# Second mixer's scores as two 64-row products in two accumulator banks, with the values' product first in each slot

## Chip, cores and metric

The kernel runs on one core of a Trainium2 chip. The metric is the device time of one execution in microseconds, taken as the median of several runs. A profiled execution of the same program gives the span and all rows shown here.

## What is computed

A trunk of two layers on a sequence of 256 tokens with 2048 channels, in fp32. Layer 0 has two parallel mixers in one projection (a gated linear recurrence, and 16 heads of windowed attention of 64 channels each), layer 1 has differential attention; after each comes a gated feed-forward part. The layer that the change is about, cut from the reference:

```python
q = z[..., :qk_w].reshape(bsz, seq, C_HEADS, 2, C_QK)        # 16 heads, 2 maps, 64 channels
k = z[..., qk_w:2 * qk_w].reshape(bsz, seq, C_HEADS, 2, C_QK)
v = z[..., 2 * qk_w:].reshape(bsz, seq, C_HEADS, C_V)        # C_V = 128
s = jnp.einsum('bqhje,bkhje->bhjqk', qblk, k)                # one score matrix per map j
p = jax.nn.softmax(s, axis=-1)
att = p[:, :, 0] - lam * p[:, :, 1]
return jnp.einsum('bhqk,bkhe->bqhe', att, v)
```

## The kernel before

**Large products.** Every weight block of 512 x 512 passes through two forms: ScalarE writes its high part (`hi`, line 1051), VectorE the rest (`lo`, line 1791). TensorE then forms three products (high by high, low by high, high by low). A *slot* is one such block: two halves (one per tile of 128 tokens) of 12 products of 512 columns, 24 in all (`product`, line 1461, matmul on line 1477). The two banks of each of two accumulator pairs `acc` take turns.

**Order of the work.** `make_plan` writes one list of tasks, and each engine's program walks through that list and picks out what is its own, so the list is the order on TensorE, VectorE, ScalarE, GpSimd and the load queue alike. `run` (line 332) makes for each slot: the first half, `early` tasks, `hi` and `lo` of blocks to come, in the output projection an `add_output` per half (VectorE adds the product to the sum in SBUF, lines 1909 and 1911), the second half, and then the `post` tasks.

**Attention within the slots.** `mixer_slots` (line 204) spreads the heads over slots. A group has 8 of them, i = 0 to 7. In layer 0 there are 2 groups (16 heads); in layer 1 there are 4 groups, and one i is one head for one tile of 128 queries, so 32. For each i, three slots one after the other hold its steps on TensorE: the score (`s0`) in slot start + i, the transposes of the softmax weights (`pt`) one slot later, the values' product (`pv`) two slots later. The groups start at slots that lie 10 apart in layer 0 and 10 or 12 apart in layer 1; the last group of either layer lies in the slots of the output projection. Lines 260 to 265 give the order within a slot:

```python
for s in range(len(slots)):
    for kind, lag in (("s0", 0), ("pt", 1), ("pv", 2), ("s", 0)):
```

**The steps of layer 1.** The score is one product (line 1590): the stationary operand is 128 rows of queries (64 channels of map 0, 64 of map 1), and the moving one is 128 rows by 512 columns of keys, where map 0's keys stand in the upper 64 rows of the first 256 columns and map 1's in the lower 64 rows of the last 256, with zeros in the other two quarters (`keys`, zeroed by GpSimd, line 2312). It fills the bank `sc`. VectorE takes the maximum of both maps in one reduce (line 1927) and scales it (line 1929); ScalarE forms the two exponentials from `sc` into `prob` (line 1152) and counts `exp_done`; VectorE divides and subtracts the maps (`difference`, early in the next slot, lines 1937 to 1942). `pt` transposes `prob`, ScalarE copies that to `probT` (line 1164), `pv` multiplies it with the values into 128 columns of the bank `pv` (line 1619), and VectorE copies these out (line 1961, counts `o_done`). ScalarE squares them for the norm of the head (line 1174).

**The steps of layer 0.** The score is two products of 256 columns, one per tile of queries, both in `sc` (line 1586). VectorE adds the log counts and takes the maximum (line 1922, counts `s_free`). The values' product is 4 small products (line 1614); VectorE takes a reciprocal (line 1953) and scales twice into `tok` (line 1956, the second counts `o_done`).

**What a score waits for.** On TensorE a score waits for `exp_done` (layer 1) or `s_free` (layer 0) of the head before, so that `sc` has been read. A values' product waits for the copy to `probT` and for `o_done` of the head before. An fp32 product appears in the trace as two weight loads and two matmul records; a transpose as one.

**Other users of the two banks.** `sc` and `pv` are also used by the recurrence's gates, by the transposes at the boundaries between parts and by the feed-forward blocks (`corner`, `upper`, line 807); for these nothing changes.

Of the kernel before, what the change touches and what calls it, by code (L numbers as in the profile page):

```python
# [183 lines left out]
class Plan:  # L184
# [3 lines left out]
    def __init__(self):  # L188
        self.u = self.n = self.e = self.m = self.heads = self.ropes = 0
        self.stats = self.squares = self.updates = self.xm = 0  # L190
        self.y_gains, self.y_counts = {"pool": 0, "dve": 0}, {}
        self.source = {}
        self.ready, self.read, self.pt, self.parts = {}, {}, {}, []
        self.stat, self.update, self.squared, self.y_gained = {}, {}, {}, {}
        self.bodies = 0
        self.place, self.after, self.heads_of, self.head_units, self.x_read, self.wholes, self.last_body = {}, {}, [], [], [], {}, []
        self.last_ups = []

# [5 lines left out]
def mixer_slots(plan, layer):  # L204
# [53 lines left out]
    if layer == 1:  # L258
        starts[0] = evacs["k", 0].s + 3
    for s in range(len(slots)):  # L260
        for kind, lag in (("s0", 0), ("pt", 1), ("pv", 2), ("s", 0)):
            for g, start in enumerate(starts):
                i = s - start - lag
                if 0 <= i < HEADS_OF_GROUP:
                    task = put(s, kind=kind, g=g, i=i, n=plan.heads + HEADS_OF_GROUP * g + i, v_group=evacs["v", g].n)
                    if kind == "pt" and layer == 1:
                        slots[s].early.append(Task("difference", n=task.n))
# [184 lines left out]
def number(plan, tasks):  # L452

    for task in tasks:
        if task.kind == "T":
            task.e = plan.e
            plan.e += 1
            if task.src != "x":
                plan.read["tok" if task.src == "tok" else "stage", task.t] = task.e
            key = {"x": ("x", task.b), "tok": ("y", task.layer)}.get(task.src, (task.src, task.layer))  # L460
            plan.ready[(*key, task.g, task.t)] = task.e
            plan.source[(*key, task.g, task.t)] = task
            if task.src == "tok":
                task.m = plan.m
                plan.m += 1
            if task.src == "x":
                task.m = plan.xm
                task.update = plan.update.get((task.b, task.g, task.t))
                plan.xm += KT
        elif task.kind == "pt":  # L470
            task.e = plan.e
            plan.e += 1
            plan.pt[task.n] = task.e
        elif task.kind in ("rms_x", "rms_y"):
            task.stat, task.sq = plan.stats, plan.squares
            plan.stat[task.kind, task.b, task.t] = plan.stats
            plan.stats += 1
        elif task.kind in ("square", "y_square"):
            task.sq, task.update = plan.squares, plan.update.get((task.b, task.c, task.t))
            task.stat = plan.stat.get(("rms_x", task.b - 1, 0))  # L480
            plan.squares += 1
            if task.kind == "y_square":
                plan.squared[task.b, task.slot.cb, task.t] = plan.squares
        elif task.kind == "y_gain":
            task.sq, task.gained = plan.squared[task.b, task.c, task.t], plan.y_gains[task.what]
            plan.y_gained[task.b, task.c, task.t] = task.what, plan.y_gains[task.what]
            plan.y_gains[task.what] += 1
            plan.y_counts[task.b] = dict(plan.y_gains)
        if task.kind in ("evac", "silu"):
            task.stat = plan.stat["rms_x", task.b, 0]  # L490
        if task.kind == "update":
            if task.b:
                task.stat, task.update = plan.stat["rms_y", task.b, task.t], plan.updates
                task.m = plan.y_gained[task.b, task.c, task.t]
                plan.update[task.b, task.c, task.t] = plan.updates
                plan.updates += 1
        if task.kind in ("evac", "update", "pv", "s", "silu", "gate_up"):
            task.tok_free = [plan.read.get(("tok", t)) for t in range(NT)]
            task.stage_free = [plan.read.get(("stage", t)) for t in range(NT)]
        if task.kind == "s":  # L500
            task.prev_pt = plan.pt.get(task.n - 1)
        if task.kind == "half" and not task.slot.recurrent:
            region, kg = task.slot.lhs
            key = ("x", task.slot.b) if region == "h" else ("y", task.slot.layer)
            if region == "h" and task.slot.b == 0:
                task.m, task.hi = KT * (kg + 1), "xT"
            elif task.slot.w == "down":
                task.e, task.m = task.slot.block_e + task.t, task.slot.block_m + task.t
            else:
                turn = plan.source[(*key, kg, task.t)]  # L510
                task.e, task.m, task.hi = turn.e, turn.m, turn.src
# [118 lines left out]
def trunk(nc, x, norm_mix_pre, norm_mix_post, norm_ffn_pre, norm_ffn_post,  # L630
# [9 lines left out]
    with ExitStack() as ctx:  # L640
# [78 lines left out]

        acc = [[ctx.enter_context(nc.psum_tensor(f"acc{i}{t}", [P, KC], F32)) for t in range(NT)] for i in range(2)]  # L720
        tp = [ctx.enter_context(nc.psum_tensor(f"tp{i}", [P, KT, P], F32)) for i in range(2)]
        sc = ctx.enter_context(nc.psum_tensor("sc", [P, 2, T], F32))
        pv = ctx.enter_context(nc.psum_tensor("pv", [P, 2, T], F32))


        landed = [sem(f"landed{i}") for i in range(BLOCK_RAW)]
# [292 lines left out]
        def _(act):  # L1019
# [119 lines left out]
            def softmax(task):  # L1139
                n = task.n  # L1140
                act.wait_ge(nmx_done, n + 1)
                if n >= 2:
                    act.wait_ge(o_done, n - 1)
                if task.layer == 0:
                    for t in range(NT):
                        ins = act.activation(prob[:, t, :], prob[:, t, :], ACT.Exp, scale=SCALE, bias=nmx[:, t:t + 1],
                                             accum_out=den[n % 2][:, t:t + 1])
                    ins.then_inc(exp_done, 1)
                else:
                    act.wait_ge(tp_done, task.prev_pt + 1)  # L1150
                    for m in range(2):
                        ins = act.activation(prob[:, m, :], sc[:, m, :], ACT.Exp, scale=SCALE, bias=nmx[:, m:m + 1],
                                             accum_out=den[n % 2][:, m:m + 1])
                    ins.then_inc(exp_done, 1)

# [278 lines left out]
        def _(pe):  # L1434
# [75 lines left out]
            def task_of(task):  # L1510
# [60 lines left out]
                elif task.kind == "s0":  # L1571
                    n = task.n
                    if n > 16:
                        pe.wait_ge(exp_done, n)
                    elif n:
                        pe.wait_ge(s_free, n)
                    else:
                        pe.wait_ge(rg_act, RG_ACT * (AT - 1) + 4)
                    if task.i == 0:
                        for src in "qk":  # L1580
                            for t in range(NT):
                                wait_event(pe, plan.ready[src, task.layer, task.g, t])
                    q, k, kt = qT[task.g % 2], keys[task.g % 2], task.i // 2
                    if task.layer == 0:
                        for t in range(NT):
                            mm = pe.matmul(sc[:, t, :], q[:, kt, t * P:(t + 1) * P], k[:, kt, task.i % 2, :],  # L1586
                                           start=True, stop=True)
                    else:
                        t = task.i % 2
                        mm = pe.matmul(sc[:, :, :].rearrange("p m t -> p (m t)"), q[:, kt, t * P:(t + 1) * P],  # L1590
                                       k[:, kt, :, :].rearrange("p m t -> p (m t)"), start=True, stop=True)
                    mm.then_inc(s_done, 1)
                elif task.kind == "pt":
                    if task.layer == 0:
# [7 lines left out]
                elif task.kind == "pv":  # L1602
                    n = task.n
                    wait_event(pe, plan.pt[n])
                    if n:
                        pe.wait_ge(o_done, n)
                    if task.i == 0:
                        for t in range(NT):
                            wait_acc(pe, task.v_group, t)
# [152 lines left out]
        def _(dve):  # L1762
# [150 lines left out]
            def softmax(task):  # L1913
# [4 lines left out]
                if task.layer == 0:  # L1918
                    if n:
                        dve.wait_ge(tp_done, task.prev_pt + 1)  # L1920
                    for t in range(NT):
                        ins = dve.tensor_tensor_reduce(prob[:, t, :], sc[:, t, :], logc[:, t, :], 1.0, 3.0 * NEG,
                                                       ALU.add, ALU.max, mx[:, t:t + 1])
                    ins.then_inc(s_free, 1)
                    dve.wait_ge(s_free, n + 1)
                else:
                    dve.tensor_reduce(mx, sc[:, :, :], AX.X, ALU.max).then_inc(max_part, 1)
                    dve.wait_ge(max_part, n - 16 + 1)
                dve.tensor_scalar(nmx, mx, -SCALE, None, ALU.mult).then_inc(nmx_done, 1)

# [467 lines left out]
```

## Time and profile before

| | |
|---|---|
| Median of 3 runs | 2159.02 us (2158.26 to 2159.08) |
| The profiled execution's own time | 2158.62 us |
| Its span in the trace | 2156.8 us, so 1.8 us lie around it |
| TensorE busy | 2141.2 us (99%), 9771 matmuls |
| VectorE busy | 1698.2 us (79%) |
| ScalarE busy | 1489.6 us (69%) |
| GpSimd busy | 230.7 us (11%) |
| Read from memory | 416.92 MB, 196 GB/s over the span |

Layer 0's heads run from about 199 to 341 us, layer 1's from 1141 to 1435 us. Busy time of TensorE is the sum of its matmul records; these overlap (a record lasts from the entry of its first column to the exit of its last), so a duration there is longer than the step from one matmul to the next. The chain of waits, in which each piece ends where the next begins, shows the steps.

### The profile page before, as it was taken

How to read it: one execution, taken by the hardware profiler on the slowest of the kernel's cores; microseconds unless marked ns; L12 is line 12 of the kernel's file. 1: busy time of each engine (PE TensorE's matmuls, PEld its weight loads, DVE VectorE, ACT ScalarE, POOL GpSimd, SP SyncE). 2: the span in 40 equal slices, each digit the busy share in tenths (PEclk: the TensorE clock that was granted, in tenths of full speed). 3: DMA queues.
4: the chain of work that ended last, by engine and by line, in shares of the span. 5: the costliest groups of instructions: out<-in, count | busy, mean ns of one | idle time of the engine just before them, and what ended most of it. 6: DMA issues, size and time to landing. Idle time of an engine off the chain costs nothing.

```text
span 2156.8 us, 26554 instructions
## 1 busy us (share of the span) xinstructions
PE 2141.2 (99%) x9771; PEld 1765.4 (82%) x9771; DVE 1698.2 (79%) x1538; ACT 1489.6 (69%) x1774; POOL 230.7 (11%) x274
## 2 busy tenths in 40 slices
PE   9999999999999999999999999999999999999998
PEld 7888888888888888888887787788888888888886
DVE  5577466898898888888755656678998888888886
ACT  6677544787777777777655555447777777777774
POOL 0851000000000000000021001001000000000001
PEclk9999999999999999999999999999999999999999
DMA  9545445799989999997564454557999999998993
GB/s 315 189 154 194 145 148 198 255 290 298 266 256 263 282 296 276 285 289 230 183 215 146 149 169 143 177 175 239 278 299 273 275 292 279 281 292 266 263 263 149
DMA packets 226559, 508.82 MB, mean 236 GB/s; under 512 B 13736, under 2 KB 16384, under 8 KB 214656
## 3 DMA queue, kind: packets, MB, share of 16 engines
q1 hardware_dynamic: 214192, 422.68, 55.6%
q0 software_dynamic: 11520, 83.89, 19.7%
q8 instruction: 79, 1.29, 0.2%
q10 hardware_dynamic: 720, 0.56, 0.1%
q14 instruction: 48, 0.39, 0.0%
HBM read 416.92 MB, written 6.29 MB: 196 GB/s over the span
## 4 chain that ended last, share of the span: by engine, by line
PE 95%; DVE 2%; issue 1%; ACT 1%; DMA 1%; SPq 0%; ACTq 0%; POOLq 0%; POOL 0%; DVEq 0%
PE acc L1477 34%; PE acc L1696 20%; PE sc L1490 20%; PE pv L1490 10%; PE acc L1490 5%; PE tp L1504 3%; PE sc L1590 1%; DVE w_lo L1791 1%; PE pv L1619 1%; PE sc L1586 1%; PE pv L1614 1%; DMA raw<-in_ev_w_in 0%; PE sc L1569 0%; PE pv L1569 0%; ACT h_hi L1097 0%
## 5 line engine op out<-in xcount | busy, mean ns | idle before, releaser
L1791 DVE TENSOR_TENSOR w_lo<-raw,w_hi 128x2048 fp32r<-128x2048 f32 x263 | 601.6, 2293 | 100.2 <-PE acc L1477 41.5
L1051 ACT ACTIVATE w_hi<-raw 128x2048 fp32r<-128x2048 f32 x263 | 503.7, 1916 | 120.4 <-PE acc L1477 45.6
L1477 PE MATMUL acc<-w_hi,h_hi 128*128 128x512 f32 x936 | 261.4, 401 | 2.6 <-ACT h_hi L1021 2.6
L1477 PE MATMUL acc<-w_lo,h_hi 128*128 128x512 f32 x936 | 252.2, 391 | 0.2
L1477 PE MATMUL acc<-w_hi,h_lo 128*128 128x512 f32 x936 | 251.1, 390 | 0.0
L1791 DVE TENSOR_TENSOR w_lo<-xs,w_hi 128x2048 fp32r<-128x2048 f32 x88 | 201.2, 2288 | 31.3 <-PE acc L1696 20.4
L1477 PEld LDWEIGHTS acc<-w_lo,h_hi 128*128 128x128 f32 x936 | 175.6, 188 | 38.9 <-DVE w_lo L1791 1.4
L1477 PEld LDWEIGHTS acc<-w_hi,h_lo 128*128 128x128 f32 x936 | 175.5, 188 | 37.0
L1477 PEld LDWEIGHTS acc<-w_hi,h_hi 128*128 128x128 f32 x936 | 171.1, 189 | 37.0 <-issue 5.5
L1051 ACT ACTIVATE w_hi<-xs 128x2048 fp32r<-128x2048 f32 x88 | 168.5, 1915 | 23.9 <-PE acc L1490 8.1
L1317 ACT ACTIVATE yacc<-acc 128x512 f32<-128x512 f32 x160 | 95.0, 595 | 113.3 <-PE acc L1696 113.3
L1696 PE MATMUL acc<-w_hi,y_lo 128*128 128x512 f32 x640 | 171.0, 389 | 0.0
L1696 PE MATMUL acc<-w_hi,y_hi 128*128 128x512 f32 x640 | 171.0, 389 | 0.0
L1696 PE MATMUL acc<-w_lo,y_hi 128*128 128x512 f32 x640 | 171.0, 389 | 0.0
L1791 DVE TENSOR_TENSOR w_lo<-gq,w_hi 128x2048 fp32r<-128x2048 f32 x54 | 123.5, 2288 | 24.4 <-PE acc L1696 19.6
L1696 PEld LDWEIGHTS acc<-w_hi,y_hi 128*128 128x128 f32 x640 | 120.1, 188 | 24.9
L1696 PEld LDWEIGHTS acc<-w_lo,y_hi 128*128 128x128 f32 x640 | 120.1, 188 | 24.9
L1696 PEld LDWEIGHTS acc<-w_hi,y_lo 128*128 128x128 f32 x640 | 120.1, 188 | 24.9
L1791 DVE TENSOR_TENSOR w_lo<-queries,w_hi 128x2048 fp32r<-128x2048 f32 x50 | 114.4, 2287 | 15.5 <-PE acc L1696 10.2
L1051 ACT ACTIVATE w_hi<-gq 128x2048 fp32r<-128x2048 f32 x54 | 103.5, 1917 | 23.6 <-DVE gq L1804 11.6
L1791 DVE TENSOR_TENSOR w_lo<-gx,w_hi 128x2048 fp32r<-128x2048 f32 x46 | 105.2, 2288 | 15.6 <-PE acc L1696 10.2
L1490 PE MATMUL sc<-w_hi,h_hi 128*128 128x512 f32 x400 | 108.9, 394 | 0.0
(299 smaller groups left out, 3615.6 us busy)
## 6 DMA issues: line engine op xcount, KB each, us to landing
raw<-in_od_w_in SPq DMA_DIRECT2D x48, 1024.0 KB, 5.1
raw<-in_ffn_w_gate SPq DMA_DIRECT2D x38, 1024.0 KB, 9.7
raw<-in_ev_w_in SPq DMA_DIRECT2D x37, 1024.0 KB, 5.3
raw<-in_ffn_w_up SPq DMA_DIRECT2D x36, 1024.0 KB, 7.8
raw<-in_ffn_w_down SPq DMA_DIRECT2D x36, 1024.0 KB, 6.6
xs<-in_ffn_w_up SPq DMA_DIRECT2D x22, 1024.0 KB, 8.0
xs<-in_ffn_w_down SPq DMA_DIRECT2D x18, 1024.0 KB, 7.2
xs<-in_ffn_w_gate SPq DMA_DIRECT2D x18, 1024.0 KB, 10.2
```

Of the source, the lines that this page charges most:

```text
L1051: act.activation(w_hi[u % HI][:, :, :], raw[place.buf][:, :, :], ACT.Copy).then_inc(hi_done, 1)
L1317: act.activation(yacc[:, t, j * KC:(j + 1) * KC], down_banks[k], ACT.Copy).then_inc(drained[k], 1)
L1477: mm = pe.matmul(acc[n % 2][t][:, :], operand(lhs, a, k, t), w[:, k, :], start=first and k == 0 and j == 0, stop=last and k == KT - 1 and ...
L1490: mm = pe.matmul(bank, a[:, k, :], w[:, k, :], start=start and k == 0 and j == 0, stop=stop and k == KT - 1 and j == 2, skip_group_check=c ...
L1504: ins = pe.transpose(dst, src, ident[:, :])
L1586: mm = pe.matmul(sc[:, t, :], q[:, kt, t * P:(t + 1) * P], k[:, kt, task.i % 2, :], start=True, stop=True)
L1590: mm = pe.matmul(sc[:, :, :].rearrange("p m t -> p (m t)"), q[:, kt, t * P:(t + 1) * P], k[:, kt, :, :].rearrange("p m t -> p (m t)"), sta ...
L1614: mm = pe.matmul(pv[:, 0, t * HD:(t + 1) * HD], probT[:, j, t * P:(t + 1) * P], v[:, j, task.i * HD:(task.i + 1) * HD], start=j == 0, stop ...
L1619: mm = pe.matmul(pv[:, 0, 0:CV], flat_pt[:, j * P:(j + 1) * P], v[:, j, hd * CV:(hd + 1) * CV], start=j == 0, stop=j == 1)
L1696: mm = pe.matmul(down_banks[k], a[:, kt, t * P:(t + 1) * P], w[:, kt, :], start=body.first and i == 0 and kt == 0, stop=i == 2 and kt == K ...
L1791: dve.tensor_tensor(w_lo[u % LO][:, :, :], raw[plan.place[u].buf][:, :, :], w_hi[u % HI][:, :, :].bitcast(F32), ALU.subtract).then_inc(lo_ ...
```

## The change

It takes `sc` and `pv` as the halves of one tensor of two banks, `heads`, and puts layer 1's score of map 0 in the first half of the first bank and that of map 1 in the second half of the second bank (`heads[:, 0::3, :]`). The values' product stays in the first 128 columns of the second bank. The score of layer 1 becomes two products, one per map, each of 64 rows by 256 columns; layer 0's score stays as it is. In each slot the order becomes values, transposes, score, in both layers. A score now also waits until all values' products issued before it have been copied out (`o_done`), and a values' product until all scores issued before it have been read (`exp_done` in layer 1, `s_free` in layer 0); the counts come from `number`.

```diff
@@ mixer_slots
-        for kind, lag in (("s0", 0), ("pt", 1), ("pv", 2), ("s", 0)):
+        for kind, lag in (("pv", 2), ("pt", 1), ("s0", 0), ("s", 0)):
@@ number
+        elif task.kind == "s0":
+            task.m = plan.products
+            plan.scores += 1
+        elif task.kind == "pv":
+            task.m = plan.scores
+            plan.products += 1
@@ trunk
-        sc = ctx.enter_context(nc.psum_tensor("sc", [P, 2, T], F32))
-        pv = ctx.enter_context(nc.psum_tensor("pv", [P, 2, T], F32))
+        heads = ctx.enter_context(nc.psum_tensor("heads", [P, 4, T], F32))
+        sc, pv = heads[:, 0:2, :], heads[:, 2:4, :]
+        scores = heads[:, 0::3, :]
@@ softmax, ScalarE
-                        ins = act.activation(prob[:, m, :], sc[:, m, :], ACT.Exp, scale=SCALE, bias=nmx[:, m:m + 1],
+                        ins = act.activation(prob[:, m, :], scores[:, m, :], ACT.Exp, scale=SCALE, bias=nmx[:, m:m + 1],
@@ TensorE, s0
+                    if task.m:
+                        pe.wait_ge(o_done, task.m)
...
-                        mm = pe.matmul(sc[:, :, :].rearrange("p m t -> p (m t)"), q[:, kt, t * P:(t + 1) * P],
-                                       k[:, kt, :, :].rearrange("p m t -> p (m t)"), start=True, stop=True)
+                        for m in range(2):
+                            rows = slice(m * HD, (m + 1) * HD)
+                            mm = pe.matmul(scores[:, m, :], q[rows, kt, t * P:(t + 1) * P], k[rows, kt, m, :],
+                                           start=True, stop=True)
@@ TensorE, pv
+                    if task.layer == 1:
+                        pe.wait_ge(exp_done, task.m)
+                    else:
+                        pe.wait_ge(s_free, task.m)
@@ softmax, VectorE
-                    dve.tensor_reduce(mx, sc[:, :, :], AX.X, ALU.max).then_inc(max_part, 1)
+                    dve.tensor_reduce(mx, scores, AX.X, ALU.max).then_inc(max_part, 1)
```

## Rows read from the trace of the kernel before

**Rows 1.** The page: busy time, the granted clock by slice, the chain that ended last.

```profile
PE 2141.2 (99%) x9771; PEld 1765.4 (82%) x9771; DVE 1698.2 (79%) x1538; ACT 1489.6 (69%) x1774; POOL 230.7 (11%) x274
...
PEclk9999999999999999999999999999999999999999
...
PE 95%; DVE 2%; issue 1%; ACT 1%; DMA 1%; SPq 0%; ACTq 0%; POOLq 0%; POOL 0%; DVEq 0%
```

**Rows 2.** Busy time by stretch: layer 0's heads, layer 1's last group, and five stretches' sum.

```profile
206.00:335.00 129.00, 128.93 (x676) 109.71 (x675) 74.00 (x157) 65.20 (x108) 9.71 (x17) 1.00 0.46 155
...
1365.00:1440.00 75.00, 74.79 (x345) 59.35 (x344) 56.48 (x99) 35.57 (x70) 1.65 (x1) 1.00 0.53 182
sum 414.00, PE 413.51 PEld 335.89 DVE 254.60 ACT 219.69 POOL 37.05; mean PE 82.70 PEld 67.18 DVE 50.92 ACT 43.94 POOL 7.41
```

**Rows 3.** The chain in order of time, layer 1: start us, us, what.

```profile
1399.80 0.86 PE sc L1590 x2
1400.65 0.22 PE tp L1504 x2
1400.87 0.45 PE pv L1619 x4
1401.32 5.48 PE acc L1477 x24
1406.80 0.86 PE sc L1590 x2
```

**Rows 4.** The chain in order of time, layer 0 (transposes left out as shorter).

```profile
228.29 0.86 PE sc L1586 x4
229.59 0.84 PE pv L1614 x8
230.43 5.54 PE acc L1477 x24
235.97 0.86 PE sc L1586 x4
```

**Rows 5.** Score records by line, layer 1 and layer 0: duration ns min/median/max.

```profile
L1590 PE MATMUL sc<-kz,queries x32: 590/591/595, 1210.2 to 1421.1; 128*128 128x512 f32 x32
...
L1586 PE MATMUL sc<-gx,queries x32: 377/378/382, 198.8 to 252.7; 128*128 128x256 f32 x32
```

**Rows 6.** Timeline, layer 1, ordinary slot: start us, us, what, idle before.

```profile
1254.20 0.61 PE L1619 MATMUL pv<-vb,probT 128*128 128x128 f32 x4
...
1254.85 0.29 DVE L1961 COPY tok<-pv 128x128 f32<-128x128 f32 x1 [1.49 <-PE pv L1619]
```

**Rows 7.** Timeline, where TensorE waited for a low part of VectorE.

```profile
398.41 1.08 PE L1477 MATMUL acc<-w_hi,h_lo 128*128 128x512 f32 x4
398.64 2.28 DVE L1791 TENSOR_TENSOR w_lo<-raw,w_hi 128x2048 fp32r<-128x2048 f32 x1
...
400.97 1.20 PE L1477 MATMUL acc<-w_lo,h_hi 128*128 128x512 f32 x4
```

**Rows 8.** Timeline, layer 0, ordinary slot.

```profile
229.43 1.00 PE L1614 MATMUL pv<-vb,probT 128*128 128x64 f32 x8
...
230.47 0.17 DVE L1953 RECIPROCAL small<-small 128x2 f32<-128x2 f32 x1 [3.92 <-PE pv L1614]
...
230.67 0.48 DVE L1956 TENSOR_SCALAR tok<-pv,small 128x64 f32<-128x64 f32 x2
```

**Rows 9.** Timeline, layer 1, a slot of the output projection.

```profile
1408.57 0.68 DVE L1927 TENSOR_REDUCE small<-sc 128x2 f32<-128x512 f32 x1
...
1411.60 2.29 DVE L1791 TENSOR_TENSOR w_lo<-raw,w_hi 128x2048 fp32r<-128x2048 f32 x1
...
1413.81 1.28 DVE L1911 TENSOR_TENSOR yacc<-acc,yacc 128x512 f32<-128x512 f32 x2
...
1415.36 0.29 DVE L1961 COPY tok<-pv 128x128 f32<-128x128 f32 x1 [0.27 <-PE pv L1619]
```

More of the change, by code:

```diff
@@ L194, in __init__ @@
         self.stat, self.update, self.squared, self.y_gained = {}, {}, {}, {}
-        self.bodies = 0
+        self.bodies = self.scores = self.products = 0
         self.place, self.after, self.heads_of, self.head_units, self.x_read, self.wholes, self.last_body = {}, {}, [], [], [], {}, []
```

## Prediction

> **What bounds the kernel now.** I read the profile from the top down. The page says that TensorE is busy for 99% of the span, that its clock was granted in full (9 tenths or more in every slice) and that the chain of work that ended last runs through it for 95% [rows 1]. So the first thing to ask of any edit is what it does to the line of TensorE's own instructions, and the second is whether it makes TensorE wait, which it hardly does today: in the table of the attention stretches it is busy for 128.93 of 129 us in the first mixer and 74.79 of 75 us in the last group of the second [rows 2].
>
> The chain of waits then gives the price of each piece of a slot. In the second mixer (layer 1) it reads: score 0.86 us, the two transposes 0.22, the values' product 0.45, the 24 large products 5.48, and the next score 7.00 us after the last [rows 3]. In the first mixer it is 0.86, then 0.44 (the gap 1.30 less 0.86), 0.84 and 5.54, together 7.68 [rows 4]. No gap is left between them: the order score, transposes, values was chosen so that each asks for something that was finished long before.
>
> **What the change removes and adds.** The score of layer 1 now streams 512 columns twice (an fp32 product is two records), with 128 rows of which half are zeros for either map: 32 scores of 0.86 us [rows 3, 5]. After the change there are four records of 256 columns: map 0 twice, map 1 twice. If they run one behind the other they cost what layer 0's two scores of 256 columns cost, four records in 0.86 us [rows 4, 5]: nothing is gained. If the two maps, which use different rows of the array and different banks, ran wholly side by side, it would be half, 0.43. The order of issue is map 0, map 0, map 1, map 1. The two records of one map need the same rows, so only the middle two can overlap: three steps of 0.86/4 = 0.215 instead of four, 0.64 us. No row shows two matmuls side by side, so this is a choice between 0.43 and 0.86, made by the order of issue. Gain 0.215 x 32 = 6.9 us, with bounds of 0 and 13.7.
>
> On overlap the Trainium skill ("TensorE: Matmul & The Clock Gate", Part 3) says that matmuls of different row groups run concurrently and still start and end in program order. By it my three steps would hold; no run here shows it.
>
> **The second bank is what costs.** Map 1's score now lies in the bank of the values' product. So a score must wait until VectorE has copied the last values' product out (o_done), and that product is now issued just ahead of it, in the same slot: values (head i-2), transposes (i-1), score (i). All 16 heads of layer 0 and all 32 of layer 1 get this order and wait. It bites only where a slot has both a values' product and a score: i = 2 to 7 of each group of 8. Groups start 10 or 12 slots apart and don't overlap, so that is 2 x 6 = 12 slots of layer 0 and 4 x 6 = 24 of layer 1. The wait that values' products get (for the exponentials of the previous slot) is met: in the old order the score waited for the same event at the same place without idling.
>
> Layer 1, ordinary slot [rows 6]: the values' product starts at 1254.20, VectorE's copy starts at 1254.85 and ends at 1255.14: 0.94 us. To hand over I take 0.05 (a low part ends at 398.64 + 2.28 = 400.92 and TensorE starts at 400.97 [rows 7]), and for the pipeline to fill again 0.13: the first group of four after an interruption takes 1.20 against 1.08, 0.12 more [rows 7], rounded up. The score so starts 1.12 us after the values' product. Without a wait it would be 0.45 + 0.22 = 0.67. Stall 0.45 us. VectorE is there in time: it idled 1.49 us before that copy, more than the 1.07 us by which the product moves forward [rows 6]. 24 - 6 = 18 such slots (the last group is below): 8.1 us.
>
> Layer 0, same way [rows 8]: values start at 229.43, the second of the two scalings ends at 230.67 + 0.48 = 231.15, so 1.72 + 0.18 = 1.90 against 0.84 + 0.44 = 1.28: stall 0.62, x 12 = 7.4 us. VectorE idled 3.92 us there, so it is ready.
>
> Layer 1, last group: its heads lie in slots of the output projection, where VectorE also adds two outputs per slot, 1.28 us, and is nearly full: it idled 0.27 us before the copy [rows 9]. With a score waiting for VectorE and VectorE's softmax waiting for the score this becomes a ring. From the start of the large products: the score ends 0.16 later (record 0.378 less step 0.215 [rows 5]), reduce from 0.20 to 0.88; 2.35 from there to the low part (1409.25 to 1411.60); 2.29; two adds 1.28; copy 0.29: 7.09. Plus 0.18, the score starts at 7.27, where without a wait it would be 5.48 + 0.67 = 6.15. Stall 1.12 x 6 = 6.7 us; bounds are 0.45 and 1.12.
>
> What is queued behind the waiting score on TensorE is the next slot's 24 products, so every stall moves the span one for one. Behind them VectorE and ScalarE wait for products, and they have room: 254.60 and 219.69 us busy of 414 us [rows 2]. ScalarE's square now goes ahead of its copy of the transposed weights; the copy is needed only a slot later. VectorE's reduce reads two half banks in place of one, still 512 elements, 0.68 us. No DMA is moved; the loads have a share of 0.45 to 0.53 [rows 2]. These edits I cost at nothing.
>
> **Sum.** Stalls 8.1 + 7.4 + 6.7 = 22.2 us, less 6.9: +15.3 us on the profiled execution's 2158.6 us (span 2156.8 and 1.8 around it), which is 0.4 below the median of the runs, 2159.0. Forecast 2174.3 us against the median, 0.7% slower. Bounds of the stalls: 16.0 us (last group at 0.45, handovers 0.06 shorter in all 36) and 25.8 us (handovers 0.1 longer); less 13.7 to 0: 2161 to 2185 us, before the rival below adds to it.
>
> **Rivals.**
> A. The two products do not overlap, or changing the array's shape costs as much as overlap brings. Then the change doesn't do what it says: 22.2 us remain, 2181 us. If leaving the 64-row shape means that the next product starts only when the last has left the array, each score pays 0.378 - 0.215 = 0.16 us [rows 5], 32 x 0.16 = 5.2, and with the overlap 15.3 + 5.2 = 20.5: 2179.5 us. For it: no row shows an overlap. Against it: the two banks would let them. The Trainium skill states such a rule ("TensorEngine Tiling (Array Packing)", Key Properties): changing the tiling mode drains TensorE. It speaks against this change; the trace of before has no change of mode around these scores to bear it out. Chance 0.36.
> B. Full overlap, 0.43 a score: 22.2 - 13.7 = +8.5, 2167.5 us. Chance 0.12.
> C. Faster: the wait on the copy is covered after all (the copy's 0.94 us shrinks, or the score's weights and first columns go in before it is met), so the overlap is kept. It decides at an average stall of 6.9/36 = 0.19 us over the 36 slots, or 13.7/36 = 0.38 with full overlap. With no stall at all the time is 2152.1 us (2145.3 with full overlap). Against it: the copy's end is read from rows, and it lies 0.27 us behind the point at which the score would start (0.94 against 0.67), before any handover; in layer 0 it lies 0.44 behind (1.72 against 1.28). Chance of faster 0.07. That the two cancel to within 0.2%: 0.09.
>
> **How the numbers follow.** My case 0.36, A 0.36, B 0.12, C 0.07, cancelled 0.09. Mine comes first by the order of issue; A beside it shifts the time only by 5 to 7 us. The range from 2163 to 2187 holds my case, A with its bounds and most of B, and leaves out C, the cancelled case and a corner on each side. 0.2% (4.3 us) is about what a measurement of this kernel can tell. All of mine, A and B are slower by more: 0.84.
>
> **What would show it.** In the changed kernel's chain, a slot of layer 1 should show values 0.45, transposes 0.22, then a hole of 0.45 us released by VectorE's copy, then four score records over 0.64 us (0.86: A; 0.43: B), then 5.48; the period grows from 7.00 to about 7.24. Layer 0's should grow from 7.68 to 8.30, and the last group's to about 7.9. The waits of TensorE, now a few us in all, should name the copy (24 times) and the scaling (12 times) with some 22 us. I am wrong if TensorE shows no idle time ahead of the scores, or if those scores cost more than 0.86 us each.

## Result and profile after

The change made the kernel slower: 2175.34 us median (2174.34 to 2177.43) against 2159.01, a ratio of 1.0077 with an interval of 1.0064 to 1.009. The forecast was 2174.3 us, with a range of 2163 to 2187. The profiled execution of the changed kernel took 2177.43 us, 2.1 above its median, with a span of 2175.6.

The page of the changed kernel gives the busy times, and its section on the chain by engine:

```profile
PE 2144.7 (99%) x9835; PEld 1766.0 (81%) x9835; DVE 1702.7 (78%) x1538; ACT 1489.6 (68%) x1774; POOL 231.6 (11%) x274
...
PEclk9999999999999999999999999999999999999999
...
PE 91%; DVE 4%; issue 2%; ACT 1%; DMA 1%; SPq 1%; POOLq 0%; POOL 0%; DVEq 0%; ACTq 0%
```

TensorE has 64 matmul records more (four instead of two for each of 32 scores), its clock is the same, and its share of the chain has fallen from 95% [rows 1] to 91%: some of the path now lies on VectorE and in handovers ("issue"). The share busy still reads 99%, which shows how little that figure says about a loss of 0.8%.

The chain in order of time shows where, for an ordinary slot of layer 1 (first) and of layer 0 (second):

```profile
1242.72 0.46 PE heads L1634 x4
...
1243.20 0.30 DVE tok L1976
1243.50 0.14 issue
1243.63 0.70 PE heads L1601 x4
1244.34 5.67 PE acc L1484 x24
...
1250.00 0.46 PE heads L1634 x4
```

```profile
233.22 0.02 issue
233.25 0.18 DVE small L1968
...
233.44 0.49 DVE tok L1971 x2
233.93 0.14 issue
234.07 1.10 PE heads L1595 x4
235.17 5.47 PE acc L1484 x24
240.64 0.85 PE heads L1629 x8
```

The transposes have left the chain: they run while VectorE copies. From one values' product to the next it is 7.28 us in layer 1 (1242.72 to 1250.00), where it was 7.00 [rows 3] and 7.24 were forecast; in layer 0 the score comes every 8.27 us (234.07, then 242.34), where it was 7.68 [rows 4] and 8.30 were forecast.

The waits of TensorE, in the order the answer has them (us in total, times, longest):

```profile
PE heads L1601 <- DVE tok L1976: 7.5, 23, 0.6
PE heads L1595 <- DVE tok L1971: 4.6, 11, 0.4
```

The two copies are named 23 and 11 times, of 24 and 12 forecast. The totals, 12.1 us, are less than the stalls, since a matmul's record lasts until its last column is out: of a hole of half a microsecond in the issue some 0.2 us are covered by the record before.

The starts of the first scores split the span (after the durations in ns stand the first and the last start in us). The first score of layer 0 started at 198.8 us [rows 5]; in the changed kernel, layer 0 and then layer 1:

```profile
L1595 PE MATMUL heads<-gx,queries x32: 377/379/454, 201.7 to 260.5; 128*128 128x256 f32 x32
```

```profile
L1601 PE MATMUL heads<-gx,queries x64: 376/414/480, 1150.9 to 1356.2; 64*128 64x256 f32 x64
```

And layer 1's first score in the kernel before:

```profile
L1590 PE MATMUL sc<-gx,queries x32: 590/591/595, 1141.2 to 1341.1; 128*128 128x512 f32 x32
```

Of the 18.8 us that the span is longer, 6.8 lie between the two first scores (949.2 against 942.4), 9.1 behind layer 1's first (1024.7 against 1015.6), and 2.9 ahead of layer 0's first score, where no instruction of the change has run yet. There TensorE waited longer for the parts of the first blocks. That this one execution lies 2.1 us above its median fits it, and in the experiments' traces layer 0's first score starts anywhere from 198.6 to 201.2 us.

### The profile page after: what moved, and what is told of

It reads as the page before. It is cut to its first block, busy times and chain, and to the rows that moved or that the text cites. A ratio compares the mean times of both kernels' runs of the same rounds, so it can differ in the third digit from the quotient of the medians.

```text
span 2175.6 us, 26729 instructions
## 1 busy us (share of the span) xinstructions
PE 2144.7 (99%) x9835; PEld 1766.0 (81%) x9835; DVE 1702.7 (78%) x1538; ACT 1489.6 (68%) x1774; POOL 231.6 (11%) x274
## 4 chain that ended last, share of the span: by engine, by line
PE 91%; DVE 4%; issue 2%; ACT 1%; DMA 1%; SPq 1%; POOLq 0%; POOL 0%; DVEq 0%; ACTq 0%
PE acc L1484 32%; PE heads L1497 29%; PE acc L1711 20%; PE acc L1497 5%; PE tp L1511 2%; DVE w_lo L1806 2%; DMA raw<-in_ev_w_in 1%; PE heads L1601 1%; PE heads L1595 1%; PE heads L1576 1%; PE heads L1629 1%; PE heads L1634 1%; DVE tok L1976 0%; ACT h_hi L1104 0%; DVE tok L1971 0%
## 5 line engine op out<-in xcount | busy, mean ns | idle before, releaser
L1497 PE MATMUL heads<-w_hi,lefts 128*128 128x512 f32 x640 | 171.0, 389 | 0.0
L1497 PEld LDWEIGHTS heads<-w_hi,lefts 128*128 128x128 f32 x640 | 120.1, 188 | 24.9
L1497 PE MATMUL heads<-w_hi,h_hi 128*128 128x512 f32 x480 | 130.2, 393 | 0.0
L1497 PE MATMUL heads<-w_lo,h_hi 128*128 128x512 f32 x480 | 128.6, 390 | 0.2
```

The lines of the kernel that those rows point to most:

```text
L1497: mm = pe.matmul(bank, a[:, k, :], w[:, k, :], start=start and k == 0 and j == 0, stop=stop and k == KT - 1 and j == 2, skip_group_check=c ...
```

## Experiments

Theory 1 is the forecast's: a score's wait for the copy of the values' product costs some 22 us, and three steps in place of four give 6.9 back. Theory 2 came out of the trace of the changed kernel: four 64-row records of a score fill only 0.70 us, too little for the forecast's steps (two of 0.215 and a last record of 0.378, 0.81), while the next matmul starts late. By it the maps overlap wholly and the array stands empty whenever its shape changes; its prices, some 0.2 us for each entering and leaving, are read from those records, and its rivals are that the order, the banks or the splitting as such made the difference.

**Layer 0 undone.**

```diff
-        for kind, lag in (("pv", 2), ("pt", 1), ("s0", 0), ("s", 0)):
+        for kind, lag in (("pv", 2), ("pt", 1), ("s0", 0), ("s", 0)) if layer else (("s0", 0), ("pt", 1), ("pv", 2), ("s", 0)):
...
-                    if task.m:
+                    if task.m and task.layer == 1:
...
-                    else:
-                        pe.wait_ge(s_free, task.m)
```

> Layer 0 gets its old order (score, transposes, values) and no wait for the copy; layer 1 stays as changed. Theory 1 (the forecast: a score's wait for the copy of the values' product costs the time) takes layer 0's share away: 12 stalls of 0.62 us, 7.4 us less than the change's 2175.3, 2167.9. Rival (layer 0's order costs nothing, and the time went elsewhere, for example into the start of the run, where the profiled execution of the change lost 2.4 us): 2173 to 2175.

Measured: 2168.18 us (2167.65 to 2171.95), ratio to before 1.0047 (1.0034 to 1.006). Layer 0's share is 7.2 us (forecast 7.4), for an edit that gives layer 0 nothing: its scores stay in one bank.

**The order and the waits with one 128-row product**, with its own bank (the arguments of the products are shortened here and below).

```diff
-        scores = heads[:, 0::3, :]
+        scores = heads[:, 0:2, :]
...
-                        for m in range(2):
-                            rows = slice(m * HD, (m + 1) * HD)
-                            mm = pe.matmul(scores[:, m, :], q[rows, ...], k[rows, kt, m, :], ...)
+                        mm = pe.matmul(sc (512 columns), q[:, ...], k[:, kt, :, :], ...)
```

> The change's order and waits, but layer 1's score is again one product of 128 rows and 512 columns in one bank (the waits are then not needed, and are kept). Theory 1 (three steps of 0.215 us in place of four for each of 32 scores): 6.9 us more than the change, 2182.2. Theory 2 (read in the records of the changed kernel: the two maps run side by side in 0.46 us, but the array stands empty for 0.2 us when its shape changes, on entering and on leaving, and the entering is covered only where TensorE waited anyway, 24 of 32 scores): 24 x 0.2 = 4.8 us more, 2180.1. Rival (the 64-row form brings nothing): 2175.3.

Measured: 2180.74 us (2180.57 to 2182.34), ratio 1.0103 (1.0089 to 1.0117): the 64-row form gives 5.4 us, between theory 2 (4.8) and theory 1 (6.9); the traces, from layer 1's first to its last score, give 6.1 (295.4 less 289.3), so this run doesn't tell the two apart. The rival (nothing) is out. Its chain in an ordinary slot, and two scores of the last group:

```profile
1241.72 0.30 DVE tok L1974
1242.02 0.14 issue
1242.16 1.10 PE heads L1599 x2
1243.26 5.49 PE acc L1484 x24
1248.75 0.46 PE heads L1632 x4
...
1411.28 1.11 PE heads L1599 x2
...
1419.28 1.11 PE heads L1599 x2
```

The score reads 1.10 us here and 0.86 in [rows 3]: 0.24 us for the array to fill after the wait. The period is 7.51 us, so the wait costs 0.51 us in an ordinary slot. In the last group it is 8.00 (1411.28 to 1419.28), so there the wait costs 1.00.

**The change with all 128 rows in each map's product**, in its two banks.

```diff
-                            mm = pe.matmul(scores[:, m, :], q[rows, kt, ...], k[rows, kt, m, :],
+                            mm = pe.matmul(scores[:, m, :], q[:, kt, ...], k[:, kt, m, :],
```

> The change's order, waits and banks, but each map's product takes all 128 rows. Theories 1 and 2 have the gain come from the rows and so give what the one product of 512 columns gives, 2182.2 and 2180.1. If the gain came from splitting into two products as such, this stays at the change's 2175.3.

Measured: 2181.11 us (2180.87 to 2181.41), ratio 1.0101 (1.0082 to 1.0119). Splitting the score into two products and two banks gives nothing; what gain there is comes from the rows.

**The order alone**, without the waits.

```diff
-                    if task.m:
-                        pe.wait_ge(o_done, task.m)
...
-                    if task.layer == 1:
-                        pe.wait_ge(exp_done, task.m)
-                    else:
-                        pe.wait_ge(s_free, task.m)
```

The rest is as in the run with one 128-row product.

> The change's order in both layers, with layer 1's score as one product of 128 rows in its own bank, and without the two new waits, which nothing then needs: the order alone. Theory 2 (the wait costs): nothing of the 22 us is left; only where a slot also turns new queries or keys, the transposes of the weights now come sooner after them and wait for ScalarE's copy, 1 to 2 us in all, so 2160 to 2161. Rival (the order costs): the run with the same order and the waits had 2180.7, this stays above 2175. What lies between the two runs is the price of the waits, forecast at 22.2 us.

Measured: 2159.66 us (2158.67 to 2161.57), ratio 1.0005 (0.9996 to 1.0014), no difference that can be told. Between 2180.74 and 2159.66 lie only the waits: 21.1 us, forecast 22.2. In the two traces the waits make 7.4 us between layer 0's first and last score, and 14.1 between layer 1's (forecast 14.8).

**Values' product in mid-slot**, so that no score has to wait. Product and copy move from `post` to the end of `early`.

```diff
                     if kind == "pt" and layer == 1:
-                        slots[s].early.append(Task("difference", n=task.n))
+                        slots[s].early.insert(0, Task("difference", n=task.n))
+                    if kind == "pv" and layer == 1:
+                        slots[s].early.append(slots[s].post.pop())
```

Layer 0 is as before the change.

> Layer 0 as before the change. In layer 1 the values' product and its copy move from the end of the slot to its middle, so that the copy is long done when the score, still two products of 64 rows in two banks, asks for it: no stall. Theory 1 (0.215 us gained per score): 2159.0 - 6.9 = 2152.1. Theory 2 (without a stall the entering of the 64-row shape costs its 0.2 us too, and a score comes to 0.84 us against 0.86): 2158.5. Rival (the order itself, not the wait, cost the time): above 2163.

> As the run with the values' product in mid-slot, but each map's product takes all 128 rows (the rows of the other map hold zeros), so the array keeps its shape and nothing can overlap. Its four records should take 0.86 us. Both theories: 2159.0. What this run shows is the difference to the 64-row form in the same order: 6.9 us by theory 1, 0.5 us by theory 2. If moving the values' product costs something by itself, it shows here as time above 2159.

Measured: 2163.54 us (2162.04 to 2164.64) with 64 rows and 2162.81 (2162.34 to 2167.02) with 128; ratios 1.0019 (1.001 to 1.0028) and 1.0019 (1.0011 to 1.0028). Without the stall the 64-row form gives nothing: theory 1's 6.9 us are refuted. But neither reaches 2159, so something else costs 4 us. The chain of the 128-row form names the greater part, in a slot that also turns new queries:

```profile
1248.42 0.45 PE tp L1513 x4
1248.87 0.02 issue
1248.89 0.61 ACT queries L1137
1249.50 0.14 issue
1249.63 0.41 PE tp L1513 x2
1250.04 0.86 PE heads L1602 x4
```

Eight transposes of queries (the chain has the last part of them) fill both transpose banks. The weights' transposes now follow at once and wait for ScalarE to empty one of them; before, the score of 0.86 us stood in between. With the values' product in between, as in the change, the wait for the queries' copy is gone. All waits of TensorE in this run between 1141 and 1440 us:

```profile
PE tp L1513 <- DVE h_lo L1822: 1.1, 1, 1.1
PE tp L1513 <- ACT queries L1137: 1.0, 3, 0.3
PE tp L1513 <- ACT kz L1145: 0.9, 1, 0.9
```

So ScalarE has 1.9 us of it, and 1.1 us is a single wait for VectorE, at the start of the last group, where the transposes need a bank that VectorE has yet to read (the next expectation puts that one down to ScalarE). Before the change these waits were 0.2 us; in the order alone, and in the change beside its waits for the copy, they are 1.6.

**Mid-slot values, and the score ahead of the transposes again.**

```diff
-        ... (("pv", 2), ("pt", 1), ("s0", 0), ("s", 0)) ...
+        ... (("pv", 2), ("s0", 0), ("pt", 1), ("s", 0)) ...
```

> Values' product and copy in mid-slot, and now the score ahead of the transposes again, as before the change; scores of 64 rows in two banks. The run with the transposes first was 4.4 us above the kernel before, and its trace shows 0.55 us more in each slot that also turns queries or keys, and 1.5 us at the start of the last group, where the transposes wait for ScalarE's copy out of the transpose bank. If that is the cause, these 4.4 us go: 2158.5 by theory 2 (a score of two shapes' changes costs 0.84 us against 0.86). Theory 1 (0.215 us gained per score) says 2152.1. If moving the values' product costs by itself: 2163.

> As the run before it in this job, with 128 rows in each map's product: no change of shape, no overlap. 2159.0 by both theories; the difference to the 64-row form is 0.5 us by theory 2 and 6.9 us by theory 1.

Measured: 2159.22 us (2157.74 to 2162.52) with 64 rows and 2160.5 (2159.19 to 2161.97) with 128; ratios to before 1.0002 (0.9993 to 1.0011) and 1.0007 (0.9998 to 1.0016). Putting the score ahead of the transposes takes the 4 us away, and with no stall left the two forms lie 1.3 us apart, which the spread of the runs doesn't separate from the 0.5 of theory 2, and which is far from 6.9. The traces are finer: an ordinary slot takes 6.97 us with 64 rows and 7.03 with 128 in two products, where one product of 128 rows took 7.00 [rows 3], and from layer 1's first to its last score it is 279.0, 280.9 and 279.4 us. So the 64-row form keeps 0.06 us per slot against the same two products with 128 rows, and 0.03 against the kernel before. This is the changed idea without its cost, and it only equals the kernel before. The timeline of the two around one score, 64 rows first; its second line is the same view cut off 0.15 us into the score, which shows the records that have started by then:

```profile
1226.95 0.70 PE L1603 MATMUL heads<-kz,queries 64*128 64x256 f32 x4
1226.95 0.49 PE L1603 MATMUL heads<-kz,queries 64*128 64x256 f32 x2
1227.58 0.20 PEld L1513 LDWEIGHTS tp<-ident,prob 128*128 128x128 f32 x2 [0.33 <-issue]
```

```profile
1226.20 1.02 PE L1602 MATMUL heads<-kz,queries 128*128 128x256 f32 x4
```

Four records stand within 0.70 us instead of 1.02, but the weight loads of what follows wait 0.33 us. The records start in pairs: the first two 0.006 us apart, the other two 0.32 us later, again 0.006 us apart.

**The maps parted by the transposes**: four changes of shape per slot in place of two.

```diff
-        (("pv", 2), ("pt", 1), ("s0", 0), ("s", 0))
+        (("pv", 2), ("s0", 0), ("pt", 1), ("s1", 0), ("s", 0))
...
+                elif task.kind == "s1":
+                    pe.matmul(scores[:, 1, :], q[HD:P, kt, ...], k[HD:P, kt, 1, :], ...).then_inc(s_done, 1)
```

> As the run with the values' product in mid-slot (no stall), but the two 64-row products of a score are parted: map 0, then the two transposes of 128 rows, then map 1. In 28 slots the array changes its shape four times in place of two, and no maps overlap. Theory 2 (0.2 us for each entering and leaving): 2 x 0.43 + 4 x 0.2 = 1.66 us against 0.86 us, 28 x 0.8 = 22 us above 2159, 2181. Theory 1 (no cost of a change of shape): four records one behind the other, 0.86 us, 2159. If only leaving costs: 28 x 0.4 = 11 us, 2170.

Measured: 2181.61 us (2180.94 to 2182.54), ratio 1.0103 (1.0087 to 1.0119), as theory 2 has it. The chain of this run, then of the run with both maps together and the score first:

```profile
1238.95 0.63 PE heads L1601 x2
1239.58 0.37 PE tp L1513 x2
1239.94 0.63 PE heads L1606 x2
1240.57 2.96 PE acc L1486 x12
```

```profile
1227.02 0.63 PE heads L1603 x4
1227.65 0.37 PE tp L1513 x2
1228.02 2.78 PE acc L1486 x12
```

One map alone takes 0.63 us, and both together take 0.63 us: the second map is free. In the run with the maps parted, the two records of one map start 0.32 us apart, so neither of the pairs above can be of one map: each holds a record of either map. Of the 0.63, two records of 256 columns stream for 0.43 ([rows 4]: four in 0.86); so 0.20 us go on entering. The transposes behind read 0.37 where they are 0.22 in [rows 3], and the large products 2.96 in place of 2.78: leaving costs 0.15 to 0.18. Parting the maps costs 0.63 + 0.18 = 0.81 us per slot, of which 0.43 is the lost overlap and 0.38 the added pair of changes; times 28 it is 22.7 us, and the run lies 22.6 above before. The rows show that the weight load of the next shape starts late (the 0.33 us above). Whether that load alone is held back or the whole array has to be empty, they don't show. (Here the first map stands between the query transposes and those of the weights, as the score did before the change.)

## Why the prediction was right, and where it was not

**The wait** was the right mechanism and the right size. The run with layer 0 undone gives 7.2 us for it (forecast 7.4), the order with and without the waits 21.1 us for all of them (22.2). An ordinary slot of layer 1 costs 0.51 us, not 0.45: the score's columns flow 1.16 us after the values' product begins (0.92 in the chain and 0.24 to refill), where I had 1.12; the rest is rounding.

**The ring of the last group** is real, and my price for it was too high. The changed kernel's chain there:

```profile
1409.82 0.72 PE heads L1601 x4
1410.56 0.70 DVE small L1942
...
1413.60 2.29 DVE w_lo L1806
1415.88 0.83 DVE yacc L1926 x2
1416.72 0.28 issue
1417.00 0.29 DVE tok L1976
1417.43 0.72 PE heads L1601 x4
```

TensorE's large products don't appear in it at all: VectorE sets the pace, 7.61 us a slot, forecast 7.9. From the end of the low part to the copy it takes 1.11 us, not 1.28. The two adds are as long as before:

```profile
1415.80 1.28 DVE L1926 TENSOR_TENSOR yacc<-acc,yacc 128x512 f32<-128x512 f32 x2
1417.00 0.28 DVE L1976 COPY tok<-heads 128x128 f32<-128x128 f32 x1
```

But they start 0.09 us before the low part's record ends (1415.80 against 1415.89), and the copy starts 0.08 before theirs ends; I had added whole durations one behind the other. The score takes 0.74 to the reduce, not 0.84, and the handover 0.14, not 0.18. With one product of 128 rows in the ring the wait costs 1.00 us per slot, where I had 1.12.

**The gain** is the step that failed. I took three steps of 0.215 us, since the two records of one map need the same rows; the sum, 0.645 in place of 0.86, happened to be nearly what the chain then showed. I had taken the order of issue to be the order in which the records run; the pairs 0.006 us apart show that it isn't. In fact the maps overlap wholly (0.43), as rival B had it, and the changes of shape cost 0.20 and 0.15 to 0.18, of which rival A had the second. Behind a stall the entering is hidden in the refill, and an ordinary slot keeps 0.22 us (7.51 less 7.28). In the last group's ring it keeps 0.39 (8.00 less 7.61): the reduce starts when the score ends, 1.11 us after its start with one product and 0.72 with the 64-row ones, and the leaving isn't on VectorE's path. Without a stall nearly nothing is kept. So 24 of the 32 scores gained, 18 x 0.22 + 6 x 0.39 = 6.3 us, where the traces give 6.1 and the medians 5.4. That this lies so near my 6.9, and the 0.22 so near my 0.215, is luck: no slot gains by three steps. What I named as the sign of each case, the length of the score in the chain, would have read 0.70 as my own; I also had to ask how late the next product starts.

By the Trainium skill ("TensorEngine Tiling (Array Packing)", Key Properties) a change of the tiling mode drains TensorE; the traces agree, with 0.20 us in and 0.15 to 0.18 out. By the Trainium skill ("TensorE: Matmul & The Clock Gate", Part 3) matmuls of different row groups run concurrently; two maps in the 0.63 us of one agree. The three steps that I drew from its program order didn't come.

**The order** cost nothing that can be told (0.9 us, with an interval across zero), as I had it. What I did not see is that the score also covered ScalarE's copy between two groups of transposes; the change kept about half of that cover by chance, with the values' product in its place: its transposes wait 1.6 us where those of the kernel before waited 0.2, and 3.0 with nothing in between.

**The sum.** By the medians it is 21.1 for the waits, 0.9 for the order, less 5.4: 16.6 us, measured 16.3. That closes by construction, since the three are differences of the same medians. A count by slots doesn't: 12 slots of layer 0 at 0.59 us (8.27 less 7.68), 18 of layer 1 at 0.28 (7.28 less 7.00) and 6 at 0.61 (7.61 less 7.00) make 15.8 us, and the two stretches of the traces made 6.8 + 9.1 = 15.9. The forecast of 15.3 came so close partly because its misses differ in sign: the waits were 1.1 us cheaper, the gain 1.5 smaller, and the order, put at nothing, reads 0.9.

## What to carry to other kernels

Sharing a bank turns two independent steps into a chain, and on an engine that never idles every such wait costs what other work doesn't cover of the other engine's read (here 0.5 to 0.6 us each time, 1.0 where that engine was itself full), against which a saving of 0.2 to 0.4 us in the product is small; place the producer half a slot earlier before you place it next to its reader. And weigh 64-row products by pairs of changes of shape: they halved 0.86 us of streaming and gave back almost all of it, so here they paid only where the array was idle anyway. Whether they pay where many stand together was not tried.

## What the runs showed that was not expected

- The two maps' four records overlap in pairs: one map or both take 0.63 us. Each pair has a record of either map, though the program issues both records of map 0 first; which record of a map is in which pair, and what puts them in this order, isn't shown.
- Entering the 64-row shape costs 0.20 us and leaving it 0.15 to 0.18 us. After a wait the first is free, since a 128-row score pays 0.24 us to refill as well; in the last group, where VectorE sets the pace, the second is free too, and a 64-row score gave 0.39 us.
- No run was faster than the kernel before. Whether several scores in a row, sharing one change of shape, would be was not tried; it would need more accumulator banks than the two that scores have here.
